# A bias table from step masks: 96 small matmuls become 24 wide ones in column groups, turned by transpositions

## What is computed

```
def conformer_conv_mixer(h, w_in, conv_w, conv_b, ln_g, ln_b, w_out):
    val, glu_gate, z = split(h @ w_in, 3)
    u = causal_depthwise_conv(val * sigmoid(glu_gate), conv_w) + conv_b
    u = silu(layer_norm(u, ln_g, ln_b))
    return (u * silu(z)) @ w_out

bias = rel_bias[t5_bucket(q_pos - k_pos)]     # 32 buckets, 8 heads
logits = q . k * scale + bias
```

## Time and profile before

| | |
|---|---|
| median of 3 runs | 1857.71 us (1856.68 to 1860.08) |
| the profiled execution, its own time | 1859.46 us |
| its span from the first to the last instruction | 1857.6 us |
| PE busy | 1806.4 us, 97% of the span |
| DVE, ACT, POOL busy | 1452.4 us, 1066.9 us, 316.4 us |
| mean granted clock of PE | 0.989 |

### The profile page before, as it was taken

The page is one execution under the profiler, slowest core; times in us unless marked ns, Lnnn a source line. Parts: engine busy times, 40 slices in busy tenths (PEclk is TensorE's granted clock), DMA queues, the critical chain, the costliest instruction groups (busy, mean ns, idle before and its releaser), DMA issues.

```text
span 1857.6 us, 31518 instructions
## 1 busy us (share of the span) xinstructions
PE 1806.4 (97%) x11884; PEld 1642.6 (88%) x11884; DVE 1452.4 (78%) x2781; ACT 1066.9 (57%) x2046; POOL 316.4 (17%) x412
## 2 busy tenths in 40 slices
PE   8999999999999999999999999999999999999997
PEld 8989878878899999899997988889998998889996
DVE  8997677887878788889878697687877687687767
ACT  5887565555554444478765455455555555455554
POOL 1997000000000000089830000020000200020000
PEclk9999999999999999998999999999999999999998
DMA  6444459865558888543454553446764443446552
GB/s 223 137 134 141 146 168 313 274 214 169 170 184 288 297 290 292 197 154 122 132 167 159 183 203 103 148 153 199 238 205 159 148 148 102 148 153 205 189 183 78
DMA packets 92743, 339.66 MB, mean 183 GB/s; under 512 B 10288, under 2 KB 10672, under 8 KB 91952
## 3 DMA queue, kind: packets, MB, share of 16 engines
q1 hardware_dynamic: 92592, 337.64, 54.9%
HBM read 336.55 MB, written 1.05 MB: 182 GB/s over the span
## 4 chain that ended last, share of the span: by engine, by line
PE 67%; DVE 16%; ACT 8%; issue 6%; POOL 2%; DMA 1%; SPq 0%; DVEq 0%; ACTq 0%; POOLq 0%
PE ps L103 65%; DVE wl L119 5%; ACT tmp L109 3%; DVE ps L129 3%; POOL B L119 2%; DVE B L119 2%; PE ps L106 2%; ACT wh L112 2%; DVE tmp L119 1%; ACT B L109 1%; DVE B L124 1%; ACT XS L112 1%; ACT ps L109 1%; ACT os L112 1%; DVE X L129 0%
## 5 line engine op out<-in xcount | busy, mean ns | idle before, releaser
L103 PE MATMUL ps<-XS,wh 128*128 128x256 f32 x4464 | 825.5, 287 | 8.5 <-DVE wl L119 7.5
L103 PEld LDWEIGHTS ps<-XS,wh 128*128 128x128 f32 x4464 | 703.5, 192 | 18.6 <-issue 9.0
L119 DVE TENSOR_TENSOR wl<-raw,wh 128x1024 fp32r<-128x1024 f32 x481 | 590.8, 1256 | 144.9 <-ACT wh L112 143.8
L103 PE MATMUL ps<-XS,wl 128*128 128x256 f32 x2232 | 633.3, 284 | 0.0
L112 ACT CAST wh<-raw 128x1024 fp32r<-128x1024 f32 x481 | 485.7, 1044 | 144.0 <-PE ps L103 137.8
L103 PEld LDWEIGHTS ps<-XS,wl 128*128 128x128 f32 x2232 | 429.4, 192 | 0.1
L119 POOL TENSOR_TENSOR B<-B,tmp 128x237 f32<-128x237 f32 (+11 forms) x384 | 274.7, 758 | 670.3 <-ACT tmp L109 670.3
L103 PE MATMUL ps<-wh,os 128*128 128x512 f32 x864 | 283.9, 394 | 9.1 <-DVE os L119 6.8
L129 DVE SCALAR_TENSOR_TENSOR ps<-B,C,ps 128x254 f32<-128x254 f32 (+16 forms) x544 | 211.8, 469 | 16.9 <-ACT ps L109 16.1
L103 PEld LDWEIGHTS ps<-wh,os 128*128 128x128 f32 x864 | 162.4, 188 | 47.7 <-DVE os L119 10.9
L103 PE MATMUL ps<-B,raw 128*128 128x256 f32 x832 | 191.1, 391 | 0.0
(11 more groups left out here) (152 smaller groups left out, 1737.2 us busy)
## 6 DMA issues: line engine op xcount, KB each, us to landing
raw<-in_w SPq DMA_DIRECT2D x628, 512.0 KB, 4.5
B<-in_ln SPq DMA_DIRECT2D x4, 1024.0 KB, 7.5
C<-in_cst SPq DMA_DIRECT2D x1, 1102.5 KB, 10.3
X<-in_x SPq DMA_DIRECT2D x2, 512.0 KB, 5.8
out_x<-X SPq DMA_DIRECT2D x4, 256.0 KB, 2.5
cb<-in_cb SPq DMA_DIRECT2D x1, 512.0 KB, 13.0
pos<-in_pos SPq DMA_DIRECT2D x1, 160.0 KB, 2.3
raw<-in_w SPq DMA_DIRECT2D x1, 128.0 KB, 3.1
```

The lines of the kernel that those rows point to most:

```text
L103: return NOTHING if self.e is None else self.e.matmul(*a, **k)
L119: return NOTHING if self.e is None else self.e.tensor_tensor(o, a, b, op)
```

## The change

Masks and steps trade places on PE. A mask is now 128x512: the same 32 buckets by 4 keys on the partitions, and four groups of 128 queries as columns, for keys that lie four apart. DVE makes it by one tensor_tensor from two broadcast views (`masks`); for this the starts of the buckets are added to the key positions once (`dve_bias_begin`). `pe_bias(pe, e, bank)` loads the steps (32 columns) as weights and streams a mask through them, four times, with the outputs on partitions 0, 32, 64 and 96 of one bank: four column groups. All four masks of a portion are waited for ahead of the first matmul. The result has keys and heads on the partitions and queries in the columns. So it is copied by ACT to `G` (`act_bias_out`), turned by four transpositions of PE into the same bank (`pe_bias_turn`), and copied by ACT to its place as before (`act_bias`).

The places change too. `bias_at(j)` names the pair behind which PE multiplies a portion: in `a0` p = 1 and 4 (e = 1, 2), in `a1` p = 1, 3 and 5 (e = 3, 4, 5). ACT's copy out stands in iteration p of the same number, in its middle. PE's transpositions stand behind pair p + 1, and ACT's last copy in the middle of iteration p + 1. Portion 0 stands ahead of the normalisation of `a0` on PE and on ACT. `c` has no portion any more and 14 filler matmuls in place of 6, `b` has no masks, and in `a1` DVE makes 4 of the masks within iteration 2.

```
 def pe_entry(self, pe, L, normed):
-    if L == "c":
-        self.pe_bias(pe, 16, 7)
-    self.warm(pe, {"a0": 0, "a1": 14, "b": 18, "c": 6, "m0": 0, "m1": 20}.get(L, 18))
+    self.warm(pe, {"a0": 0, "a1": 14, "b": 18, "c": 14, "m0": 0, "m1": 20}.get(L, 18))
 ...
 def pe_a(self, pe, j):
     if j == 0:
-        self.pe_bias(pe, 16, 6)
+        self.pe_bias(pe, 0, 6)
+        self.pe_bias_turn(pe, 0, 6)
 ...
     for p in range(8):
         pair("g", p)
         pair("v", p)
-        if p in (1, 2, 4, 5):
-            self.pe_bias(pe, 8, 3)
+        if p in self.bias_at(j):
+            self.pe_bias(pe, self.bias_at(j)[p], 3)
+        if p - 1 in self.bias_at(j):
+            self.pe_bias_turn(pe, self.bias_at(j)[p - 1], 3)
         if p >= 3:
             stats(2 * p - 6)
             stats(2 * p - 5)
 ...
 def act_a(self, act, j):
     if j == 0:
+        self.act_bias_out(act, 0, 6)
         self.act_rms(act, A, lambda tb, h: s[f"x{tb}"][0], "a_norm0", True)
         self.act_bias(act, 0, 6)
 ...
     for p in range(8):
         items(p, 0, 4)
         ...
-        if p in (2, 5):
-            self.act_bias(act, (4 if j else 1) + (p == 5), 3)
         ...
         items(p, 14, 18)
+        if p in self.bias_at(j):
+            self.act_bias_out(act, self.bias_at(j)[p], 3)
+        if p - 1 in self.bias_at(j):
+            self.act_bias(act, self.bias_at(j)[p - 1], 3)
         if p:
             stats(2 * p - 2)
             stats(2 * p - 1)
 ...
 def dve_a(self, dve, j):
-            self.masks(dve, 16)
+            self.masks(dve, 4)
 ...
-        self.masks(dve, 32)
+        self.masks(dve, 8)
+            more = 1 if j and p == 2 else 0    # a mask at four places of iteration 2
 ...
+    def bias_at(self, j):
+        return {1: 3, 3: 4, 5: 5} if j else {1: 1, 4: 2}
 ...
     def masks(self, dve, n):
-            dve.ts(self.mask(x), pf[:, q:q + 128], pf[:, T + g:T + g + 1], self.c("bstart"), ALU.subtract,
-                   ALU.is_ge).then_inc(s["mask"].up(x), 1)
+            dve.tt(self.mask(y).rearrange("p (c q) -> p c q", c=4),
+                   pf[:, q:q + 128].unsqueeze(1).to_broadcast([128, 4, 128]),
+                   pf[:, g:g + 13:4].unsqueeze(2).to_broadcast([128, 4, 128]), ALU.is_ge).then_inc(s["mask"].up(y), 1)
 ...
+    def pe_bias(self, pe, e, bank):
+        pe.wait_ge(*s["bias"]["steps"])
+        for g in range(4):
+            pe.wait_ge(*s["mask"][4 * e + g])
+        if e:
+            pe.wait_ge(*s["evac"]["bias", e - 1])
+        for g in range(4):
+            ins = pe.matmul(self.ps[bank][32 * g:32 * g + 32, :], self.c("rblk", 0, 32), self.mask(4 * e + g), start=True,
+                            stop=True)
+        ins.then_inc(s["table"].up(e), 1)
+
+    def act_bias_out(self, act, e, bank):
+        act.wait_ge(*s["table"][e])
+        if e:
+            act.wait_ge(*s["turn"]["bias", e - 1])
+        act.activation(self.bias_turned(), self.ps[bank], ACT.Identity).then_inc(s["evac"].up(("bias out", e)), 1)
+
+    def pe_bias_turn(self, pe, e, bank):
+        pe.wait_ge(*s["evac"]["bias out", e])
+        for c in range(4):
+            ins = pe.transpose(self.ps[bank][:, 128 * c:128 * c + 128], b[:, 128 * c:128 * c + 128],
+                               self.c("ident", 0, 128))
+        ins.then_inc(s["turn"].up(("bias", e)), 1)
```

More of the change, by code:

```diff
@@ L379, in __init__ @@
         self.lows = self.casts = 0
-        self.nbias = self.nmask = 0
+        self.nmask = 0
         self.adas = {}
@@ L984, in dve_a @@
                 conv_end(p - 1)
+            self.masks(dve, more)
             if p < 6:
@@ L1116, in bias_views, with mask, bias_turned @@
         return b[:, 0:3072].rearrange("p (h s) -> p h s", h=8), b[:, 3072:3072 + NPOS]
[L1118 to L1125, removed]
+    def mask(self, y):
+        return self.m["B"][0][:, y % 8 * 512:y % 8 * 512 + 512]
+    def bias_at(self, j):
+        return {1: 3, 3: 4, 5: 5} if j else {1: 1, 4: 2}
+    def bias_turned(self):
+        return self.m["G"][:, 0:512]
     def dve_bias_begin(self, dve):
@@ L1135, in dve_bias_begin @@
         dve.wait_ge(*s["bias"]["pf"])
+        dve.ts(pf[:, T:T + 64], pf[:, T:T + 64], self.c("bstart"), None, ALU.add, None).then_inc(s["bias"].up("begin"), 1)
+        dve.wait_ge(*s["bias"]["begin"])
     def masks(self, dve, n):
@@ L1141, in masks @@
         for _ in range(n):
-            x = self.nmask
+            y = self.nmask
             self.nmask += 1
-            q, g = (0, x) if x < 32 else (128, x - 32)
-            if self.mask_before(x) is not None:
-                dve.wait_ge(*s["table"][self.mask_before(x)])
-            dve.ts(self.mask(x), pf[:, q:q + 128], pf[:, T + g:T + g + 1], self.c("bstart"), ALU.subtract,
-                   ALU.is_ge).then_inc(s["mask"].up(x), 1)
-    def pe_bias(self, pe, n, bank):
+            e = y // 4
@@ L1152, in pe_bias @@
+            q, g = (0, 16 * e) if e < 2 else (128, 16 * (e - 2))
+            g += T + y % 4
+            if e >= 2:
+                dve.wait_ge(*s["table"][e - 2])
+            dve.tt(self.mask(y).rearrange("p (c q) -> p c q", c=4),
+                   pf[:, q:q + 128].unsqueeze(1).to_broadcast([128, 4, 128]),
+                   pf[:, g:g + 13:4].unsqueeze(2).to_broadcast([128, 4, 128]), ALU.is_ge).then_inc(s["mask"].up(y), 1)
+    def pe_bias(self, pe, e, bank):
         s = self.s
         pe.wait_ge(*s["bias"]["steps"])
[L1154 to L1162, removed]
+        for g in range(4):
[6 more added lines that the diff above has]
+        ins.then_inc(s["table"].up(e), 1)
@@ new lines, in act_bias_out @@
+    def act_bias_out(self, act, e, bank):
+        s = self.s
+        act.wait_ge(*s["table"][e])
[3 more added lines that the diff above has]
+    def pe_bias_turn(self, pe, e, bank):
+        s, b = self.s, self.bias_turned()
+        pe.wait_ge(*s["evac"]["bias out", e])
[3 more added lines that the diff above has]
+        ins.then_inc(s["turn"].up(("bias", e)), 1)
@@ L1167, in act_bias @@
         k0 = 64 * e if e < 2 else 128 + 64 * (e - 2)
-        act.wait_ge(*s["table"][16 * e + 15])
+        act.wait_ge(*s["turn"]["bias", e])
         act.activation(Bz[:, :, k0:k0 + 64], self.ps[bank].rearrange("p (k h) -> p h k", h=8), ACT.Identity).then_inc(
@@ L1524, in dve_b @@
                 maxima(st)
-                if 9 <= st < 13:
-                    self.masks(dve, 4)
             if st < 16:
@@ L1550, in pe_c @@
                     pe.wait_ge(*(s["evac"] if kind in "cz" else s["evacd"])["c", kind, i - 2])
-                elif kind == "z":
-                    pe.wait_ge(*s["evac"]["bias", 3])
                 for n in range(2):
@@ L1566, in act_c @@
         self.act_rms(act, "c", lambda tb, h: s["resid"]["b", tb, h], "c_norm", False)
-        self.act_bias(act, 3, 7)
         def split(i):
```

## The result

The changed kernel takes 1892.04 us (median of four executions, 1891.93 to 1892.92), the kernel before 1857.31 in the same comparison: 34.7 us more, a ratio of 1.0182 with an interval of 1.0164 to 1.0201. The profiled execution spans 1891.1 us, 33.5 more than before. The forecast was 1877, within 1865 to 1888: the sign was right, the size was not.

A forecast was written before the change was run, and what follows sets the result against it. The prediction took PE's program as the bound (busy 97% of the span). Start +5.2, first conformer +4.4, short convolution -1.2 and second conformer +10.7 sum to +19.1 us: 1877 us against the median, range 1865 to 1888.

The forecast's parts named there:

- The start: Ahead of the first conformer, ACT's squares wait for portion 0's copy and a table load: +5.2 us (1.3 to 7.8).
- the five slots of 0.85 us: At the start, a portion's four matmuls on PE, only partly side by side, take 4.3 us at half clock.
- Rival 3: A portion's four column groups run at once, so the start costs 2.6 us less: 1874 us; chance 25%.
- First conformer: In `a0`, PE's transpositions wait for ACT's copies, making `z1` later by 4.4 us (2.8 to 6.2).
- Second conformer: In `a1`, PE's waits for ACT's copies of portions 4 and 5 make `z1` later: +10.7 us (8.7 to 13).
- 4 to 7 us each but the last: PE's idle times for ACT's copy behind `v2`, `v5` in `a0` and `v2`, `v4`, `v6` in `a1`.
- Rival 5: A stall holds up the raw buffers and with them ACT and POOL, 5 to 8 us more: 1884 us; chance 15%.
- DVE's masks: In `a1`, four masks in iteration 2 (2.6 us) delay DVE, but PE needs its `wl` late enough.
- The short convolution: At the entry of `c`, PE's transpositions start 1.1 us earlier: -1.2 us with a little of the clock (-1.6 to -0.5).
- Rival 1: PE's transpositions find ACT's copy done, so stalls are taken in and PE's savings count: -9 us, 1849 us; chance 4%.
- Rival 2: PE recovers ahead of `z0`, so only the start and a little more counts: 1860 us; chance 4%.
- Rival 4: A portion's four column groups run in series, 2.5 us more at the start: 1880 us; chance 20%.

The follow-up runs named there:

- the last two late kernels: Changed kernel with later transpositions in both conformers, portion 0's copy behind the squares, 22 fillers: 1856.07 us; the same with DVE's four masks in iteration 0: 1855.48 us.
- the last experiment: Changed kernel with each portion's four matmuls done once more ahead of the real ones, all four into one column group: 1899.45 us.

## Why the prediction was right or wrong

**What bounds the kernel: right.** Shifts of PE in a conformer stayed until the end: 0.7 us more came behind the second one. That the places and not the work would cost was right too, and the kernels with later places show it.

**The start: right in kind, 2.3 us too high.** ACT's wait and the table load came as written, the latter 1.28 us at 8.97. The step that failed is the five slots of 0.85 us: the portion took 1.93 us there, not 4.3. That accounts for all of it. Rival 3 was right. The Trainium skill, page "TensorEngine Tiling (Array Packing)", section "Theoretical Speedup", gives up to 4 times for 32 columns. The trace agrees: 3.4 us against 1.0 is a factor of 3.4. My reason for choosing between the bounds, that only the second record of one group would lie beside the first of the next, was a guess about order of issue with no row behind it.

**First conformer: +6.8 for +4.4, a little above its upper bound of 6.2.** The idle times of PE behind `v2` and `v5` came as forecast; timeline of PE:

```profile
64.98 1.12 PE L106 MATMUL ps<-C,G 128*128 128x128 f32 x4 [5.38 <-ACT G L109]
65.89 9.61 PE L103 MATMUL ps<-B,raw 128*128 128x256 f32 x32
...
117.86 1.12 PE L106 MATMUL ps<-C,G 128*128 128x128 f32 x4 [6.54 <-ACT G L109]
...
122.05 8.92 PE L103 MATMUL ps<-B,raw 128*128 128x256 f32 x32
```

Portion 1's stall was taken in as forecast, and its lower clock with it: the slow `g` unit behind it (9.61 us beside 7.17) stands ahead of a wait of 6.54 us for ACT, and ACT was not late then, its iteration 4 starting at 107.36, where 105.63 of before and the start's 2.9 make 108.5. What was too small is what stands between the next stall and `g6`. Less the start's 2.9 us, the turn starts at 115.0 (forecast 114.7), takes 0.9 us (0.4), and the sums take 3.3 (1.8), since the lower clock holds through both; so `g6` starts at 119.2 and not at 116.9. The one fall of the clock charged behind it came (8.92 us for `g6`), and what PE gets back until `z1` was 3.5 us for 3.6. ACT waited for sums here as well, 2.76 and 1.23 us behind portion 2. The sign "`z1` of `a0` about 10 us later" came true (ACT's copy of it at 166.80 for 157.13), but by luck: the error of the start and this one cancel.

**Second conformer: the step that failed.** It is the chain from "Portion 4: copy out at 857.34 + 0.65" on, with "ACT itself is late by some 2 us". I took ACT's iterations as fixed at 17.5 us and let only PE wait. They took 20.2 to 21.5, because the squares wait for the sums that the change had put behind PE's waits. I had written that sums of pair p need the squares of iteration p - 2, and had not turned the question round: who waits for the sums. Nor did I price portion 4's matmuls, which wait 2.80 us for ACT's last copy of portion 3 and carry the sums with them. The sign "4 to 7 us each but the last" failed too: behind `v4` PE stood idle for 1.92 us only, because PE came to it 14.3 us later in the stage than before (870.23 us, where `v4` ended at 846.60 before) while ACT's copy stood 4.8 later. With the sums ahead of the bias work, the stage measured +10.7, the number forecast, and its later events fell where the forecast had them. Rival 5 (ACT held up, 5 to 8 us more) was the nearest in size and in kind, but had the wrong carrier: of ACT's added waits 16.0 us were for sums and 6.1 for raw buffers. The raw waits follow from the sums': with the sums ahead of the bias work one of 1.05 us is left in the same part of the stage.

**DVE's masks.** "DVE makes later, but PE needs its `wl` late enough" held in the changed kernel, where PE's waits in the second conformer have none for `wl`. Once PE is on time the masks are worth 2.2 us in that stage, by the windows of the last two late kernels. It is a cost that was hidden by another.

**The short convolution: -0.3 for -1.2, with the stretches around it.** Timeline of PE at its entry, beside the earlier trace rows:

```profile
542.60 3.29 PE L103 MATMUL ps<-C 128*128 128x128 f32 x28
547.80 1.06 PE L106 MATMUL ps<-C,tmp 128*128 128x128 f32 x8 [1.92 <-ACT tmp L109]
549.47 1.94 PE L106 MATMUL ps<-C,tmp 128*128 128x128 f32 x8 [0.60 <-DVE XS L129]
```

The input comes when the forecast had it: PE enters 9.7 us later than before (542.60 for 532.92), and 547.80 less this is 538.1, for 538.0. The transpositions start 0.9 us earlier in the stage, for 1.1 forecast. The part that failed is "a little of the clock" on top. The 14 fillers end 1.92 us ahead of the input, and behind this idle time the second eight transpositions take 1.94 us where the first take 1.06, at a granted clock of 0.50 from 550 to 552 us; the stretch behind them is 0.6 us longer than before. With 22 fillers PE went straight from them into the transpositions, and the second eight took 1.52 us, as before.

**The rivals.** Rival 1, the other side, would have needed PE to find ACT's copy done. In the change it did not, as argued. The kernels with all places late arrange just that, and there the first conformer does give 4.9 us, for the 4.5 which rival 1 allowed a stage; but the second gives nothing (+0.9 us at best), and neither kernel comes near 1849 us (1856.07 and 1855.48). Rival 2's recovery ahead of `z0` didn't happen: ACT waited 6.56 us for `z0` of `a0` and 11.37 for that of `a1`. Rival 4, the groups in series, is excluded: by the last experiment, and by the 1.93 us at the start where it needs 6.8.

The range was too narrow above: it took in the bounds of each row, but ACT's pace entered only through rival 5, once, and not in every iteration.

## What to carry to other kernels

When an edit makes engine A wait for B in a new place, list what stands behind that wait in A's program, and for each ask whether B, further down, waits for it. If it does, the delay comes back and repeats in every iteration, and neither engine's old pace may be used to place later events. Cheap instructions (here one-column sums, 1.7 us) are what such a circle runs through, and behind an idle time they can cost twice as much (3.4 us here, at a granted clock of 0.50); put them ahead of the wait, or put the handoff an iteration later.

## What the runs showed that was not expected

- Four float32 matmuls of 512 columns with 32 columns of weights take 0.99 us in four column groups and 3.4 in one. One alone is estimated above at 0.85, so the four are almost entirely side by side, two records each notwithstanding.
- A stall followed by one-column matmuls keeps the granted clock at 0.50 through all of them: windows of the changed kernel at portion 4's sums, the granted clock being the number behind POOL's:

```profile
850.00:855.00 5.00, 5.00 (x24) 3.34 (x23) 5.00 (x11) 0.42 (x1) 2.64 (x4) 0.50 0.00 0
855.00:860.00 5.00, 5.00 (x15) 4.09 (x16) 5.00 (x13) 4.58 (x13) 3.76 (x6) 0.55 0.00 0
860.00:864.00 4.00, 4.00 (x20) 3.54 (x19) 3.18 (x9) 2.43 (x7) 4.00 (x7) 1.00 0.44 130
```

  PE is busy without a gap from 850 on, first with bias matmuls and sums and then with full units, and the level of 2.4 GHz comes back only near 860. Outside the last 20 us of the program there are 68.0 us at the lower level, against 30.6 before.
- The order of ACT's first instructions sets which table it loads first. With a plain copy ahead of the squares the program has 29 table loads in place of 28, and the added one, 1.28 us, stands behind the copy's wait, at 8.97.
- At the start PE's work takes about twice as long as later (1.93 us for a portion beside 0.99), while the granted clock reads 1.00 there in both kernels. So the column alone doesn't tell the speed in the first microseconds; the prediction took the speed from durations, and that held.
